# Gates of the value stage loaded eight blocks at a time, in pieces of 1 KB

## What is computed

```python
act = jax.nn.gelu(jnp.einsum('tkd,td->tk', u_tab[e], xb).astype(jnp.float32)) * gw
return jnp.einsum('tk,tkd->td', act.astype(xb.dtype), v_tab[e])
```

## Time and profile before

| | us |
|---|---|
| median of 3 runs | 2034.24 (2030.78 to 2039.18) |
| profiled execution, its own time | 2032.12 |
| its span, first to last instruction | 2030.4 |
| TensorE (PE) busy | 1912.2 (94%) |
| VectorE (DVE) busy | 1356.0 (67%) |
| ScalarE (ACT) busy | 726.4 (36%) |
| GpSimd (POOL) busy | 706.6 (35%) |

### The profile page before, as it was taken

One profiled execution on the slowest core, in us unless ns is written; L12 is line 12 of the kernel. 1 busy time (PEld: TensorE's weight loads), 2 busy tenths in 40 slices (PEclk: granted clock), 3 DMA queues, 4 the chain that ended last, 5 costly groups with the idle time before them and its releaser, 6 DMA issues.

```text
span 2030.4 us, 28703 instructions
## 1 busy us (share of the span) xinstructions
PE 1912.2 (94%) x10526; PEld 1606.1 (79%) x10526; DVE 1356.0 (67%) x2554; ACT 726.4 (36%) x967; POOL 706.6 (35%) x506
## 2 busy tenths in 40 slices
PE   5999977597999999999999999999999999999998
PEld 4999544386888888888888878878888888888886
DVE  4343658465198887779679787457666666666676
ACT  3113117441234453453455345423232232232232
POOL 2001200010146665776776677433222222222221
PEclk8999987798999999999999999999999999999999
DMA  8335833631236795996898699999888888888882
GB/s 324 94 99 34 306 122 138 222 111 52 70 132 205 271 362 194 348 378 229 295 372 328 221 347 369 325 358 355 300 288 282 299 287 281 300 287 281 297 289 95
DMA packets 220530, 504.91 MB, mean 249 GB/s; under 512 B 32200, under 2 KB 100040, under 8 KB 215184
## 3 DMA queue, kind: packets, MB, share of 16 engines
q1 hardware_dynamic: 176224, 319.03, 47.6%
q0 software_dynamic: 41472, 151.01, 20.2%
q10 hardware_dynamic: 2736, 33.60, 4.0%
HBM read 426.72 MB, written 76.57 MB: 248 GB/s over the span
## 4 chain that ended last, share of the span: by engine, by line
PE 58%; DVE 4%; DMA 4%; POOL 3%; ACT 2%; SPq 1%; issue 1%; ACTq 0%; POOLq 0%; DVEq 0%
PE experts_ps L1892 33%; PE experts_ps L1871 23%; DMA u_raw<-in_uT 4%; PE experts_ps L1883 2%; POOL u_low L183 2%; ACT u_high L1960 1%; SPq L1794 1%; PE experts_ps L1859 1%; ACT token_gates L2032 0%; DVE s_vr L2213 0%; DVE whot L2217 0%; POOL gather_rows L1735 0%; DVE oN L2161 0%; DVE wb L2199 0%; DMA s_vr<-in_v_tab 0%
## 5 line engine op out<-in xcount | busy, mean ns | idle before, releaser
L1871 PE MATMUL experts_ps<-h2h,u_high 128*128 128x480 f32 x1024 | 396.1, 387 | 6.8 <-POOL u_low L183 6.8
L1892 PE MATMUL experts_ps<-s_vh,s_ah 128*128 128x512 f32 x1024 | 399.4, 390 | 3.1 <-DVE s_al L2266 3.0
L1892 PE MATMUL experts_ps<-s_vh,s_al 128*128 128x512 f32 x1024 | 399.1, 390 | 0.0
L1892 PE MATMUL experts_ps<-s_vl,s_ah 128*128 128x512 f32 x1024 | 398.9, 390 | 0.0
L183 POOL TENSOR_TENSOR u_low<-u_raw,u_high 128x1024 fp32r<-128x1024 f32 x128 | 312.0, 2438 | 229.9 <-ACT u_high L1960 173.5
L1871 PE MATMUL experts_ps<-h2h,u_low 128*128 128x480 f32 x1024 | 388.3, 379 | 0.0
L1871 PE MATMUL experts_ps<-h2l,u_high 128*128 128x480 f32 x1024 | 388.1, 379 | 0.0
L1723 POOL DMA_INDIRECT gather_rows<-in_v_tab,expert_index x128 | 160.3, 1253 | 514.3 <-DVE u_raw L2275 493.9
L1984 ACT CAST s_vh<-s_vr 128x1024 fp32r<-128x1024 f32 x128 | 134.8, 1053 | 460.2 <-PE experts_ps L1892 457.7
L2264 DVE TENSOR_TENSOR s_vl<-s_vr,s_vh 128x1024 fp32r<-128x1024 f32 x128 | 156.7, 1224 | 204.7 <-ACT s_vh L1984 204.7
L1892 PEld LDWEIGHTS experts_ps<-s_vh,s_ah 128*128 128x128 f32 x1024 | 192.5, 188 | 43.9 <-DVE s_al L2266 3.4
(11 more groups left out here) (411 smaller groups left out, 2773.6 us busy)
## 6 DMA issues: line engine op xcount, KB each, us to landing
u_raw<-in_uT SPq DMA_DIRECT2D x128, 512.0 KB, 4.6
s_vr<-in_v_tab SPq DMA_DIRECT2D x128, 512.0 KB, 5.1
scratch_HG<-s_ar SPq DMA_DIRECT2D x128, 256.0 KB, 5.7
scratch_G<-token_gates ACTq DMA_DIRECT2D x16, 2048.0 KB, 10.4
s_ar<-scratch_HG SPq DMA_DIRECT2D x128, 256.0 KB, 4.2
token_gates<-scratch_G SPq DMA_DIRECT2D x30, 1024.0 KB, 10.4
mod_first<-in_w_ada SPq DMA_DIRECT2D x4, 2048.0 KB, 9.7
wa_second<-in_w_ada SPq DMA_DIRECT2D x4, 2048.0 KB, 8.1
```

What stands on the lines that cost most here:

```text
L1871: mm = pe.matmul(hP[:, slot, 0:NDENSE], w[:, slot, k, :], x[:, k, 0:NDENSE], start=(k == 0 and w is u.high and x is m.h2h), stop=(k == KD ...
L1892: mm = pe.matmul(yP[:, y, :], a[:, s, t * P:(t + 1) * P], v[:, s, d], start=(start and a is ah and v is vh), stop=(stop and v is vl))
```

## The change

Gates are loaded for GG = 8 blocks at a time. A contiguous piece is then 8 x 32 values, 1 KB; a load has the same 2048 pieces, 2 MiB. The two buffers are twice as large and take the whole of `token_gates`, so the second lies in the half from which ScalarE copies the sixteenth part and from which the last part is stored. For that reason only the first buffer is filled during the hidden stage (one load of 15 parts instead of two, 1920 KiB in both cases) and the second after the loads of blocks 4 to 7, ahead of `res.load`. The loads of blocks 8 to 15 then follow `res.load` without gates between them; the loop starts with block 16 and has seven turns of two groups of eight. VectorE waits for gates at every eighth block. ScalarE makes one copy of 128 x 256 instead of two of 128 x 128.

```diff
+GG = 8
-    gr = flat_gate[:, 0:NKEY * HT].rearrange("p (g t n) -> p g t n", g=2, t=NHT)
+    gr = flat_gate.rearrange("p (g t n) -> p g t n", g=2, t=NHT)
...
                 def load_g(g, par, parts=NHT):
-                    at = slice(g * GB * HT, (g + 1) * GB * HT) if isinstance(g, int) else ds(g * (GB * HT), GB * HT)
+                    at = slice(g * GG * HT, (g + 1) * GG * HT) if isinstance(g, int) else ds(g * (GG * HT), GG * HT)
                     sp.dma_start(gr[:, par, 0:parts, :], Glayout[:, 0:parts, at]).then_inc(g_in[par], 16)
...
                         sp.wait_ge(g_out[1], 8 * NHT - 16)
-                        for g in range(2):
-                            load_g(g, g, NHT - 1)
+                        load_g(0, 0, NHT - 1)
...
                 sp.wait_ge(g_out[1], 8 * NHT)
+                load_g(1, 1)
                 res.load(sp, T)
-                with sp.Fori(1, NGR // 2) as i:
+                for n in range(GG, 2 * GG):
+                    load_block(n, n % GB)
+                with sp.Fori(1, NKEY // (2 * GG)) as i:
                     for par in range(2):
-                        sp.wait_ge(weighted, i * (2 * GB) + (par - 1) * GB)
+                        sp.wait_ge(weighted, i * (2 * GG) + (par - 1) * GG)
                         load_g(i * 2 + par, par)
-                        for s in range(GB):
-                            load_block(i * (2 * GB) + (par * GB + s), s)
+                        for n in range(GG):
+                            load_block(i * (2 * GG) + (par * GG + n), n % GB)
...
-                for g in range(2):
-                    act.copy(gr[:, g, NHT - 1, :], Gs[:, NKEY + g * GB:NKEY + (g + 1) * GB, :].rearrange("p j t -> p (j t)")
-                             ).then_inc(g_last, 1)
+                act.copy(gr[:, 0, NHT - 1, :], Gs[:, NKEY:NKEY + GG, :].rearrange("p j t -> p (j t)")).then_inc(g_last, 1)
...
                 def weigh_values(n):
                     g, s = n // GB, n % GB
-                    if s == 0:
-                        dve.wait_ge(g_in[g % 2], 16 * (g // 2 + 1))
-                        dve.wait_ge(g_last, min(g + 1, 2))
+                    gates_of, at = n // GG, n % GG * HT
+                    if n % GG == 0:
+                        dve.wait_ge(g_in[gates_of % 2], 16 * (gates_of // 2 + 1))
+                        dve.wait_ge(g_last, 1)
...
-                    dve.tensor_tensor(a, a, gr[:, g % 2, :, s * HT:(s + 1) * HT], ALU.mult).then_inc(weighted, 1)
+                    dve.tensor_tensor(a, a, gr[:, gates_of % 2, :, at:at + HT], ALU.mult).then_inc(weighted, 1)
```

## The result

| | before | after |
|---|---|---|
| median, 20 runs each | 2035.74 us | 2040.28 us |
| ratio | | 1.0022, 95% interval 1.0011 to 1.0032 |
| profiled execution, span | 2030.4 us | 2039.0 us |

The changed kernel is slower by 4.5 us (2.2 to 6.5 by the interval), within the 0.5% that I called the same and inside the range. I had forecast +1.4, which the interval excludes. The time is 4.7 us above the forecast 2035.6; 1.5 us of that is that the kernel before has a median of 2035.74 over 20 runs where three had given 2034.24.

A forecast was written before the change was run, and what follows sets the result against it. TensorE, busy 94% of the span, was taken as the bound, with one 4.9 us stall ahead of block 8. Queue +2.4 less 1.0 carried gave +1.4, so 2033.5 profiled; the median's 2.1 offset made 2035.6 us, range 2029 to 2043.

The forecast's parts named there:

- Part 1: Queue ahead of block 8: 2 MiB of gates at 348 GB/s instead of 1 MiB at 291 adds 2.4 us before v(8).
- Part 2: First gates in 1 KB pieces save 1.1 us of queue; U block 127 gains 0.35 us, work to v(7) about 1.0.
- half clock: TensorE's reduced clock after the stall ahead of block 8: left at 1.7 us, up to 0.7 us more.
- Sum: Start of block 8: +2.4 us of queue less 1.0 us carried forward, giving +1.4 us.
- Parts 3 and 4: Loop with 14 loads of 2 MiB, and the rest (copies, weighing stride, waits, tail): cost 0 or nothing measurable.
- rival C: Value loop: recurring stall at each group of eight, 4.9 us each, 69 us in all, time 2103; chance 0.05.
- A: Gate loads: 1 KB pieces move no faster than 512 B; price +3.6 us, time 2037.8; chance 0.13.
- B: Ahead of block 8: the stall goes, v(8) coming 3.2 us forward; price -4.9 us, time 2029.3; chance 0.07.

The follow-up runs named there:

- e2: Changed kernel with the gates of blocks 8 to 15 in two 1 MiB loads, the second after block 11's loads; ratio 1.0004 to the kernel before.
- e3: Changed kernel with the 4 MiB of res.load issued in eight portions after every second block from 16 to 30; ratio 0.9978 to the kernel before.
- e4: Kernel before with res.load issued in eight portions after every second block from 16 to 30; ratio 0.9969 to the unedited kernel before.
- e5: Changed kernel with its first gates as two loads of four blocks in 512 B pieces; first weighing 2.83 us after TensorE's restart, no ratio given.
- e7: Changed kernel loading 1 of the 15 parts of the first gates; first weighing 3.84 us after TensorE's restart, no ratio given.
- e9: Changed kernel with the gates of blocks 8 to 15 as two loads in 512 B pieces, both ahead of res.load; 36.15 us from v(7) issue to v(8) landing.
- e8: Changed kernel with the gate load of blocks 8 to 15 behind res.load instead of ahead of it; ratio 1.0013 to the kernel before.
- e1: Changed kernel run again unedited for a second profile; ratio 1.0019 to the kernel before.
- e10: Changed kernel with only res.load's repeated rows (1.5 MiB, 10 issues) delayed; 29.85 us from v(7) issue to v(8) landing, no ratio given.

## Why the prediction was right, and where it was not

**The place and the cause were right, the size was not.** The time fell inside the range, but the range was 14 us wide and would have held no change too; +1.4 us is a third of what was measured. The value stage had one stall, ahead of block 8, and the change made it longer through bytes ahead of v(8). Taking the extra load away (e2) takes the stall back; taking the queue away (e3, e4) takes all of it away in both kernels.

**Part 1, the queue term, was right.** +2.4 us forecast, +2.4 measured (34.6 against 32.2; with e5 to e7, which have the same loads ahead of v(8), 34.8, hence +2.6). Its rates hold: 350 GB/s in the trace, and e9 in one profile. By the rule of "DMA: Bandwidth & Descriptors" in the Trainium skill (section "Specifications"), pieces from 512 B on run at full rate; e9 speaks against it, with 1.35 us between pieces of 512 B and 1 KB for 2 MiB. The sentence that the place of the load doesn't matter holds: e8's difference is within the spread of the profiles when it is counted from the landing of v(7). That SyncE would be held at the first DMA of res.load came true.

**Part 2 failed.** It said that 1.1 us of saved queue time is carried from the first gates to all that follows, because the queue is full from 1294 to 1320: -1.0 us up to v(7) and -0.35 us for U block 127. Neither came in the two profiles of the changed kernel: v(7) is issued at R + 18.1 instead of R + 17.5 in the mean, and TensorE stands idle for 0.34 and 0.35 us ahead of R, as in the earlier trace rows; only e9 shows the second. A full DMA share says that the engines work, not that one line of transfers is pushed ahead. In the changed kernel about 1 us is won by R - 10 and lost again by R + 3 at full engines; in e7, where more was saved, the time before the next transfers are issued goes unused. What is worse, block 0 is later: 3.2 to 4.0 us to the first weighing in the seven profiles of the table with first gates in 1 KB pieces against 2.83 to 2.86 with 512 B, and TensorE waits 0.5 to 1.2 us for it. In e3, where no stall follows, it is paid (R to the end of the matmuls 703.0 us, 702.2 in e4); where the stall at block 8 follows, that should take it up. Why the first gates in 1 KB pieces go with later rows of block 0, which are issued 18 us after them, is open: e7, with hardly any gates, shows the same, so it isn't the gates' own traffic. The faster store beside the loads is a candidate, but e8 speaks against it: its store took 9.6 us, as in the kernel before, and TensorE still waited 0.64 us for block 0.

**The half clock was mis-sized.** I left it at 1.7 us and gave +0.7 as the upper end. Before it cost 1.6 us in three profiles with stalls of 3.2 to 3.8 us; after stalls of 5.1 to 7.0 us it cost 1.8 to 2.9, 2.9 and 2.1 in the two profiles of the changed kernel. That is +0.9. The length of the stall doesn't order these costs: e5 has 1.9 us after 6.9, e1 2.1 after 5.1.

**Sum.** +2.4 for the queue, +0.6 where -1.0 was forecast, +0.9 for the clock: 3.9 us. From R to the end of the matmuls the changed kernel took 712.8 and 709.8 us, the one before 707.1, 707.7 and 707.6: 3.8 us, and the timed runs say 4.5. The -0.35 of U block 127 lies before R and stayed away. Of the +0.6 only that it isn't -1.0 is shown: v(7) is issued at R + 17.2 to R + 17.8 before and at R + 17.2 and R + 19.0 after. Without the extra load (e2) the matmuls end at R + 708.7, without the 1 KB pieces in the first gates (e5) at R + 711.0, against 707.5 before and 711.3 after in the mean: some 2.6 of the 3.8 us hang on the load ahead of v(8). These are single profiles, and the two of the changed kernel differ by 3 us.

**Parts 3 and 4 were right.** No group of eight waited long enough to matter: over 640.5 us no idle time of TensorE, the DMA share down from 0.84 to 0.82 (0.81 forecast), the loops of e3 and e4 equal. VectorE's weighing still takes 684 ns, so the wider stride costs nothing. The landing of the changed kernel's gate loads, the answer to the earlier trace rows:

```profile
DMA to landing us min/median/max: 8.8/13.4/17.3
```

The median is 13.4 us (12.8 forecast), the slowest 17.3, far from the 35 at which rival C decides.

**The rivals.** A is excluded by 350 GB/s, and by e9 in one profile, although its price of +3.6 was nearer to the result than the forecast: the right size for a wrong reason. B needed what part 2 had promised and more; the saving isn't carried at all. C didn't happen.

## What to carry to other kernels

Look for the one place where a queue feeds a stage that has no stock, and count the bytes ahead of the first transfer that matters there; a larger transfer in a loop with 20 us of lead is free, the same transfer at such a place costs its full length. Before you carry saved DMA time forward, find what issues the next transfers: if they are issued on a computing engine's clock, the saving can end there. Check it by the landing of the transfer that matters; a full DMA share doesn't show it. What isn't needed until the end of the kernel (here 4 MiB) belongs behind the start of the stage: moving it was worth more, 0.3%, than the whole question of piece size.

## What the runs showed of the hardware

- Pieces of 512 B, 1 KB and 4 KB moved at 291, 350 and 410 GB/s with all 16 DMA engines busy, in stretches of 1 to 3 us. The line through the first and the last, 9.3 ns a piece plus 0.0368 ns a byte on one engine, gives 348 for the second.
- While eight loads of 64 KiB landed beside other traffic, full DMA engines moved 269 GB/s (before) and 283 (after).
- A gap of 0.6 us (e10) left TensorE's granted clock at 1.00 (2.4 GHz), and so did one of 1.5 us ahead of block 0 in e9 (1.00 over the 6 us behind it); gaps of 3.2 to 7.0 us were all followed by a stretch at 0.50 (1.2 GHz), which cost 1.6 to 2.9 us beyond the gap.
